# Indexer scores head by head, with query and key/value projections between the heads, and the first attention scores of layer 1 ahead of its last gate projection

## What is computed

```python
q, k, v, qi, ki, wi, z = jnp.split(h @ w_in, DSA_SPLITS, axis=-1)
q = rope(q.reshape(B, S, DSA_HEADS, DSA_HEAD_DIM), pos)      # 8 heads of 128
k = rope(k.reshape(B, S, DSA_KV_HEADS, DSA_HEAD_DIM), pos)
qi = rope(qi.reshape(B, S, IDX_HEADS, IDX_DIM), pos)         # 8 heads of 64
ki = rope(ki, pos)
logits = jnp.einsum('bqhd,bkd->bqhk', qi, k_idx) * (IDX_DIM ** -0.5)
score = jnp.einsum('bqhk,bqh->bqk', jax.nn.relu(logits), wi * (IDX_HEADS ** -0.5))
score = jnp.where(causal[None], score, -jnp.inf)
_, idx = lax.top_k(score, top_k)                             # top_k = 256
o = dsa_attention(...)        # softmax over the selected keys only
return (o * jax.nn.silu(z)) @ w_out
```

## Time and profile before

| | |
|---|---|
| time, median of 3 runs | 1346.89 us (1346.02 to 1347.38) |
| the profiled execution | 1348.37 us, its span 1346.5 us |
| PE busy | 1302.9 us, 97% of the span |
| DVE, ACT, POOL busy | 803.5, 563.1, 524.6 us |
| chain that ended last | PE 38% of the span, DVE 5%, ACT 2%, POOL 1% |
| mean granted clock of PE | 0.99 |

### The profile page before, as it was taken

How to read it: one execution, slowest core, us unless ns; L and a number is a source line. 1 busy time by engine, 2 the same in 40 slices (tenths; PEclk the granted TensorE clock), 3 DMA queues, 4 the chain that set the end, 5 groups by cost and what they waited for, 6 DMA issues and landing times. The chain is left out here.

```text
span 1346.5 us, 19019 instructions
## 1 busy us (share of the span) xinstructions
PE 1302.9 (97%) x6890; PEld 1111.5 (83%) x6890; DVE 803.5 (60%) x1581; ACT 563.1 (42%) x1134; POOL 524.6 (39%) x721
## 2 busy tenths in 40 slices
PE   9999999999999999999987999999899999999997
PEld 8878888989898888888766788888788988888885
DVE  7624755555556345245577889977977776345233
ACT  8312244554454023123235665564266666023122
POOL 2842034554443744234401132331066564744201
PEclk9999999999999999999998999999999999999999
DMA  6232331121101522133300122342222221521122
GB/s 203 77 106 78 112 116 56 55 71 48 55 32 56 175 87 75 60 96 120 95 0 1 55 87 89 110 140 67 88 72 64 79 63 64 153 95 59 60 65 87
DMA packets 83372, 110.07 MB, mean 82 GB/s; under 512 B 9552, under 2 KB 45648, under 8 KB 83280
## 3 DMA queue, kind: packets, MB, share of 16 engines
q1 hardware_dynamic: 83280, 108.86, 26.0%
HBM read 81.04 MB, written 27.79 MB: 81 GB/s over the span
## 5 line engine op out<-in xcount | busy, mean ns | idle before, releaser
L1700 PE MATMUL psum<-ring_hi,act_lo 128*128 128x512 f32 x816 | 322.4, 395 | 0.7 <-DVE act_lo L1688 0.7
L1702 PE MATMUL psum<-ring_hi,act_hi 128*128 128x512 f32 x816 | 318.9, 391 | 0.0
L1701 PE MATMUL psum<-ring_lo,act_hi 128*128 128x512 f32 x816 | 318.8, 391 | 0.0
L1126 POOL CAST ring_hi<-raw 128x512 fp32r<-128x512 f32 x128 | 81.8, 639 | 322.6 <-DMA raw<-in_dsa_w_in 144.0
L1341 DVE TENSOR_TENSOR act_lo<-psum,act_hi 128x512 fp32r<-128x512 f32 (+3 forms) x276 | 156.0, 594 | 67.2 <-ACT act_hi L1170 40.9
L1129 POOL TENSOR_TENSOR ring_lo<-raw,ring_hi 128x512 fp32r<-128x512 f32 x128 | 180.0, 1406 | 10.4
L1700 PEld LDWEIGHTS psum<-ring_hi,act_lo 128*128 128x128 f32 x816 | 154.1, 189 | 32.8 <-DVE act_lo L1688 1.4
L1702 PEld LDWEIGHTS psum<-ring_hi,act_hi 128*128 128x128 f32 x816 | 153.8, 188 | 32.3
L1701 PEld LDWEIGHTS psum<-ring_lo,act_hi 128*128 128x128 f32 x816 | 154.1, 189 | 31.0
L1170 ACT ACTIVATE act_hi<-psum 128x512 fp32r<-128x512 f32 (+1 forms) x244 | 114.9, 511 | 150.2 <-PE psum L1912 80.5
L1140 POOL TENSOR_TENSOR small<-small 128x1 f32<-128x1 f32 x128 | 70.7, 552 | 228.7 <-ACT p L1308 169.8
(11 more groups left out here) (257 smaller groups left out, 2473.7 us busy)
## 6 DMA issues: line engine op xcount, KB each, us to landing
raw<-in_dsa_w_in SPq DMA_DIRECT2D x48, 256.0 KB, 3.1
gz<-z_scratch SPq DMA_DIRECT2D x16, 512.0 KB, 3.6
raw<-in_ple_w_gate SPq DMA_DIRECT2D x32, 256.0 KB, 3.1
raw<-in_mla_w_in SPq DMA_DIRECT2D x19, 256.0 KB, 2.9
xr<-in_x_t SPq DMA_DIRECT2D x16, 256.0 KB, 6.8
z_scratch<-gz SPq DMA_DIRECT2D x16, 256.0 KB, 2.0
raw<-in_mla_w_out SPq DMA_DIRECT2D x16, 256.0 KB, 3.4
p<-in_x SPq DMA_DIRECT2D x16, 256.0 KB, 3.1
```

Source lines behind the costliest of these rows:

```text
L1126: last = nc.gpsimd.tensor_copy(dst, src[:, c0:c0 + cols])
L1700: nc.tensor.matmul(dst, lhs(1), rhs(0), start=start, stop=False)
L1701: nc.tensor.matmul(dst, lhs(0), rhs(1), start=False, stop=False)
L1702: return nc.tensor.matmul(dst, lhs(0), rhs(0), start=False, stop=stop)
```

## The change

In the indexer each head is a step of its own, with one bank (or a pair of banks over 512 keys), taken in turn from rings B and A. There are three rows for relu copies instead of two, the third in `xr`. The projection of tile t + 2 stands behind head 1 of tile t, the split of tile t + 1 behind head 5. In tiles 6 and 7, where no query projection is left, key/value projections 0 and 1 stand in that place. The rotated query rows go to a place of their own in `xr`, so `p1` is free for the key/value rows.

The search uses DVE on tiles 2, 3 and 4 and ACT on 5, 6 and 7; gate jobs 2 and 5 carry two rounds. The last step counts on DVE only for ACT's tiles. `above` is gone: ACT makes sign(threshold - score) of each tile with its sum, and DVE works the selection in three passes and one of a single column. The tiles are selected in the order 6, 4, 7, 3, 5, 2.

Key transposes of group 0 move behind gate job 12, the value split behind job 13, and behind job 14 stand two masks (in `xr`), the scores, minimum and Exp of tiles 6 and 7 of head 0 and the selection of tile 2. Gate job 15 takes its bank from ring B and writes its result to `xr` instead of to `p0`. Keys and values of layer 1 lie in halves of the activation buffer that the last gate jobs no longer read. Two weight pieces of the output projection are fetched at gate jobs 9 and 11.

```diff
-SEARCH = [2, 4, 5, 3, 6, 7]
-ACT_TILES = [3, 6, 7]
+SEARCH = [2, 3, 4, 5, 6, 7]
+ACT_TILES = [5, 6, 7]
+KV_EARLY = 2
+TWO_ROUNDS = (2, 5)
+SELECT = [6, 4, 7, 3, 5, 2]
...
+    def idx_scores(t, heads):
         keys = (t + 1) * P
-        for h in range(0, IDX_HEADS, 2):
-            wide = keys > CW
-            s = add("idx", {"b_full": 2, "relu": 2, "sc": 2}, ring="AB"[h // 2 % 2], jobs=2, freed=["relu"],
...
+        for h in heads:
+            add("idx", {"b_full": 1, "relu": 1, "sc": 1}, ring=next_ring(), jobs=1, freed=["relu"],
+                wide=keys > CW, t=t, h=h, keys=keys, q_ready=max(qi_ready[t], lo_at["kiT"]),
+                x2=now["x2_st"], gfree=read_by["G"])
...
+    qi_job(FULL + 2)
+    kv_weights(6, 7)
+    idx_scores(FULL, range(4))
+    qi_split(FULL + 1, next_ring())
+    idx_scores(FULL, range(4, IDX_HEADS))
+    add("idx_mask", None, t=FULL)
+    for t in range(FULL + 1, T):
+        idx_scores(t, range(2))
+        if t + 2 < T:
+            qi_job(t + 2, next_ring())
+        elif t - T + 2 < KV_EARLY:
+            kv_job(t - T + 2, next_ring())
+        idx_scores(t, range(2, 6))
         if t + 1 < T:
-            qi_ready[t + 1] = qi_split(t + 1, rot[t + 1])
-        if t + 2 < T:
-            rot[t + 2] = qi_job(t + 2)
-        idx_scores(t, qi_ready[t])
+            qi_split(t + 1, next_ring())
+        idx_scores(t, range(6, IDX_HEADS))
+        add("idx_mask", None, t=t)
...
-    after_bits = [("last_step", None, {}), ("above", None, {})]
-    after_bits += [("sel", {"found": 1}, {"t": t}) for t in range(FULL, T)]
+    after_bits = [("last_step", {"thr": 1}, {})]
+    after_bits += [("sel", {"found": 1, "sgn": 1}, {"t": t, "side_free": max(0, j - 1)}) for j, t in enumerate(SELECT)]
...
     def z_extra(k):
         search()
+        if k in TWO_ROUNDS:
+            search()
...
+        if k == 12:
+            for j in range(2):
+                k_ready[0] = split4("p1", 0, ("k0_ld", k0.after["k0_ld"]), dest="kT", g=0, j=j).after["lo"]
+        if k == 13:
+            first_q["next"] = t2_load("q", 1, v_prep(0, first_q["v_ld"], now["a_full"]))
+        if k in (9, 11):
+            w(chunk_of(1, 7), k // 2 - 4)
...
+        if k == 14:
+            for qb in order[:2]:
+                add("mask_first", None, t=qb)
+            for qb in order[:2]:
+                ps = att["n"] % 3
+                early.append((0, qb, e_step(s_step(1, 0, qb, max(first_q["ready"], k_ready[0]), first=True)), ps))
+            kind, incs, kw = after_bits.pop(0)
+            add(kind, incs, **kw)
+            p0_stored.extend(gate_free[j] for j in range(2))
...
+                    nc.scalar.activation(side_at(t), score_at(t), ACT.Sign, bias=u_cand.bitcast(F32)[:, i:i + 1],
+                                         scale=-1.0, accum_out=cnt[:, i:i + 1]).then_inc(sem["sgn"], 1)
...
                     linked(nc.vector.tensor_scalar(eq, score_at(t), thr, None, ALU.is_equal))
-                    linked(nc.vector.tensor_tensor_scan(order, eq, eq, 0.0, ALU.add, ALU.max))
-                    linked(nc.vector.scalar_tensor_tensor(eq, order, need[:, i:i + 1], eq, ALU.is_le, ALU.mult))
-                    nc.vector.scalar_tensor_tensor(score_at(t), score_at(t), thr, eq, ALU.is_gt,
-                                                   ALU.add).then_inc(sem["found"], 1)
+                    linked(nc.vector.tensor_tensor_scan(order, eq, eq, float(2 * keys - 4 * TOPK), ALU.add, ALU.add))
+                    dve.wait_ge(sem["sgn"], s.after["sgn"])
+                    linked(nc.vector.scalar_tensor_tensor(need[:, i:i + 1], order[:, keys - 1:keys], 0.5, cnt[:, i:i + 1],
+                                                          ALU.mult, ALU.add))
+                    nc.vector.scalar_tensor_tensor(score_at(t), order, need[:, i:i + 1], side_at(t), ALU.is_le,
+                                                   ALU.is_gt).then_inc(sem["found"], 1)
```

More of the change, by code:

```diff
@@ L260, in z_chunk @@
             else:
-                proj(lay, i, job, ["zs"], {"zs": 1, "z_st%d" % slot: 1}, slot=slot, base=base)
+                proj(lay, i, job, ["zs"], {"zs": 1, "z_st%d" % slot: 1}, slot=slot, base=base,
+                     side_read=now["found"], ring="B" if base and job == 7 else "A")
+                gate_free[slot] = now["z_st%d" % slot]
             if extra:
@@ L626, in qi_split, with qi_job @@
[L626 to L631, removed]
+    rot, qi_ready, stack_read = {}, {}, {}
+    def qi_job(t, ring="A"):
+        rot[t] = rope_job(1, 1, t, t % 2, cs=cs.after["cs_ld"], stack_read=stack_read.get(t - 2), ring=ring,
+                          x2=now["x2_st"]).after["rot"]
@@ new lines, in qi_split, with kv_job, kv_weights @@
+    def qi_split(t, ring="B"):
+        s = add("qi_split", {"b_full": 2, "hi": 2, "lo": 2}, ring=ring, jobs=2, freed=["lo"], slot=t % 2, rot=rot[t])
+        stack_read[t] = s.after["hi"]
+        qi_ready[t] = s.after["lo"]
+    def kv_job(t, ring="A"):
+        slot = t % 2
+        rope_job(1, 2, t, slot, extra_inc={"st%d" % slot: 1, "vcopy": 1}, st_before=now["st%d" % slot], ring=ring)
+    def kv_weights(*rows):
+        for d in rows:
+            w(next_chunk(1, 1), d)
+    kv_weights(0, 1)
@@ L663, in search @@
         search_end(search_begin())
-    n = 0
-    for i, name in ((2, "kv"), (3, "q"), (4, "q")):
+    for t in range(KV_EARLY, T):
+        for job in range(KV_EARLY) if t == KV_EARLY else ():
+            ahead(next_chunk(1, 2), job)
+        ahead(next_chunk(1, 2), t)
+        kv_job(t)
+        search()
+    for i in (3, 4):
         for t in range(T):
             ahead(next_chunk(1, i), t)
[L669 to L679, removed]
+            slot = t % 2
+            st = search_begin()
+            rope_job(1, i, t, slot, extra_inc={"st%d" % slot: 1}, base=(i - 3) * CW, st_before=now["st%d" % slot])
+            search_end(st)
     q_stored = (now["st0"], now["st1"])
@@ L713, in plan @@
     act_free = now["a_full"]
-    k_ready, v_ready = {}, {}
-    for j in range(2):
-        k_ready[0] = split4("p1", 0, ("k0_ld", k0.after["k0_ld"]), dest="kT", g=0, j=j).after["lo"]
-    def v_prep(g, ld, act_free):
-        s = add("v_split", {"hi": 1, "lo": 1}, g=g, ld=ld, act_free=act_free)
-        v_ready[g] = s.after["lo"]
-        return ("lo", s.after["lo"])
-    rd = v_prep(0, first_q["v_ld"], act_free)
-    waiting = []
+    ld = first_q["next"]
+    waiting = list(early)
     ready_pv = []
@@ L1667, in _ @@
                     else:
-                        nc.vector.tensor_tensor_reduce(rows[ps][:, 0:keys], src, mask_at(n["qb"]).bitcast(F32),
+                        if n["z_done"]:
+                            dve.wait_ge(sem["z_st0"], n["z_done"][0])
+                            dve.wait_ge(sem["z_st1"], n["z_done"][1])
+                        mask = mask_first(n["qb"]) if n["first"] else mask_at(n["qb"]).bitcast(F32)
+                        nc.vector.tensor_tensor_reduce(rows[ps][:, 0:keys], src, mask,
                                                        -DSA_SCALE, 3.4e38, ALU.add, ALU.min,
```

201 lines of the change are left out of this document (116 added, 85 removed).

## The result

The changed kernel takes 1349.34 us (median, 1345.91 to 1351.93) against 1347.47 us before (1346.02 to 1348.61): ratio 1.0013, 95% interval 1.0007 to 1.0018. So the changed kernel is 0.9 to 2.4 us slower, where 11.4 us less were forecast. The profiled execution took 1349.3 us, the median itself, around a span of 1347.5 us.

The account below looks back on a forecast made before the run. TensorE was taken as the bound, busy 1302.9 of 1346.5 us. Gains of 4.4 (indexer), 0 (search) and 7.0 us (head 0) sum to 11.4, giving 1335.5 us; bounds 1328.0 to 1343.5 us.

Parts of the forecast that it names:

- Part 3: Start of head 0 of layer 1's attention: PE's waits and lowered clock go, less 1.6 us new wait; -7.0 us.
- half rate: Indexer: PE waits of 2 us or more bring 3.3 us at half clock; 3.6 x 1.65 = 5.9 us.
- Part 1: Indexer, heads unpaired and two key/value projections moved among them: 10.3 us gained at full clock, -4.4 us after lowered clock.
- chain forecast: Indexer, one projection's end to the next: rotation, accumulates, split, two heads, projection; 12.9 to 15.4 us a tile.
- Part 2: Search during projections and gate jobs: PE never waits for it, DVE's last selection comes in time; 0 us.
- rival B: Search late: rounds beside Silu take 5.3 us, not 4.3, shrinking head 0's gain to 2 to 3; about 1340 us, chance 0.18.
- Rival C: Nothing to measure: five halved clocks in the indexer and a wait for row 0 in head 0; 1344 to 1349 us, 0.08.
- row chain: Head 0, from a score in PSUM to its scaled row: 4.1 us, fitting beside the last gate job's 5.44 us.
- Rivals A and D: Indexer. A: clock stays up, 1329.6 us, chance 0.20. D: lower clock covers whole projections, 1357 us, chance 0.07.

Follow-up runs that it names:

- both repairs: Changed kernel with the next tile's query split put ahead of the projection and the weight piece fetched at gate job 13; 1327.45 us, ratio 0.9851.

## Why the prediction was wrong

**Part 3 failed, and took most of the forecast.** It took the first scores, exponentials and scaling as the whole path of head 0 and asked of SP only whether the gate rows come in time for their reader ("the first output that wants them comes behind six more scores, so 0"). That is true of the reader and not of the queue. The weight piece stands behind that load on SP, and its cast stands in POOL's order between two rows that PE waits for. Rows brought forward by 6 us overtook a transfer that was pushed back by 1.7. The price is 7.3 us in head 0 (234.0 against 226.7 with the piece ahead): PE stands idle 5.0 us longer (6.9 against 2.0) and is busy 2.4 us longer (227.1 against 224.7), at half rate. Without it part 3 is worth 6.1 us where 7.0 were forecast; of new waits the forecast took 1.6 us for row 0, and there are two for splits on DVE, 0.4 and 0.6 us. Of the 6.1, only 2.3 to 2.8 are due to the early scores.

**Part 1 had the mechanism right and a term too small.** From one projection's end to the next (the first from 671.82), at the forecast's own split into chain and half rate:

| projection behind heads 0, 1 of tile | 3 | 4 | 5 | 6 | 7 |
|---|---|---|---|---|---|
| chain forecast, us | 12.9 | 14.15 | 14.7 | 15.4 | 15.4 |
| measured, us | 13.4 | 16.2 | 15.2 | 17.3 | 19.0 |
| of it half rate (half the stretch) | 0 | 1.6 | 0 | 1.6 | 3.0 |
| measured chain | 13.4 | 14.6 | 15.2 | 15.7 | 16.0 |

Each link is 0.3 to 0.6 us longer, 2.2 us in all. Of these 1.3 us are DVE's own pause between its accumulates, 0.12 us where 0.04 were taken, which the forecast named as its lower end (16 x 0.1 us) and left out. The other 0.9 lie between the projection's end and the first accumulate, 2.87 us where 2.75 were taken in four links and 2.36 for 1.95 in the last. For example, behind the projection that ends at 685.19 DVE's split begins at 691.49, 6.3 us later, where 2.75 + 3.16 = 5.9 were taken. In DVE's timeline (a row of two, with 0.12 us between):
```profile
689.82 1.64 DVE L1651 SCALAR_TENSOR_TENSOR xr<-gz,wis,xr 128x512 f32<-128x512 f32 x2
691.49 1.30 DVE L1430 TENSOR_TENSOR head_w_hi<-psum,head_w_hi 64x512 fp32r<-64x512 f32 x2
```
Half rate cost 6.2 us for 5.9 forecast, but in three stretches, one of them 6.0 us long, not in 3.6 of 3.3. So part 1 gave 2.1 us in this execution, inside its bounds of 0.4 and 10.3 us. That the half rate came out so near is luck: with the same waits PE was busy up to 3.1 us longer in the other kernels' profiles. The trace of the kernel before already spoke against the forecast's rule that a wait of 2 us or more is followed by half rate. Its four stretches are the indexer's; the wait of 2.04 us at 970.15 is followed by full rate:
```profile
971.49 0.40 PE L1700 MATMUL psum<-act_hi,kpe_lo 128*128 128x512 f32 x1
```

**What the forecast did not ask** was whether the order of the chain was needed. It worked out that the new order stands still for 14.6 us and took this as its nature. The split reads rotated rows that are there one tile earlier; ahead of the projection it costs nothing, and 13.3 us of the indexer go.

**Part 2** was right: 0, and the last selection is in time; rival B did not happen. Rival C (1344 to 1349 us at 0.08) came nearest in its number, 0.3 us below the measured time, and not in its mechanism, since part 3 did not come near its lower end of 3.0 but fell below 0, which its bounds excluded: they were drawn from the row chain alone. Rivals A and D did not happen.

Of the 1.9 us outside both parts, 0.9 lie ahead of the changed code, where the profiled executions of the kernels here vary between 664.0 and 665.6 us. The 0.9 us behind head 1's first score also stand in the experiments' profiles (354.7 to 355.3 us against 354.3); their cause was not looked for and stays open.

## What to carry to other kernels

When rows on the critical path are brought forward, list for every in-order queue that they pass, POOL and SP too, what stands between two of them, and when its transfer is issued: a cast that has always been ready is so only by the old lateness. A load that waits for a store holds everything behind it on its queue (1.7 us here); fetch what others wait for ahead of it. And where a forecast finds a chain of latencies, ask for each step when its input is there: a step whose input is a tile old can be put down ahead of the long work. The value of an edit depends on which bound is left, 0 or 5.8 us for the same two lines here.

## What the runs showed of the hardware

The same wait at the same place is followed by a half rate in one profile and not in another. PE's wait for the low half of tile 3's split, in the changed kernel and in the one with the split ahead:
```profile
679.30 0.39 PE L1973 MATMUL psum<-kpe_lo,head_w_lo 128*128 128x512 f32 x1
```
```profile
677.71 0.60 PE L1972 MATMUL psum<-kpe_lo,head_w_lo 128*128 128x512 f32 x1 [1.84 <-DVE head_w_lo L1429]
678.11 0.63 PE L1972 MATMUL psum<-kpe_hi,head_w_lo 128*128 128x512 f32 x1
```
The waits are 1.85 and 1.84 us. Ten of the profiles here have this wait; six show the half rate behind it and four do not. The wait of 2.00 us before tile 5's first head is alike: full rate in the changed kernel, half rate in the one with the piece ahead, whose next projection takes 7.0 us instead of 5.5. In the kernel with the projections behind the heads a wait of 2.49 us was followed by full rate. PE worked at half rate for 3.1 to 6.2 us behind one wait in the indexer. So a forecast of one stretch per wait of about 2 us is a chance and not a count. It fits that the changed kernel's 20 times spread over 6.0 us with mean clocks between 0.988 (slowest) and 0.992 (fastest), and that its indexer differs by 3.1 us between profiles by half rate alone. The kernel with both repairs, with few such waits, spreads over 1.8 us, but in four runs only, and the kernel before, with six waits of 1.96 to 2.93 us, over 2.6 us in 20; that the stretches make the whole spread was not tested by itself.

The table loads on ACT at the last gate job:
```profile
970.81 0.97 ACT L1245 ACTIVATE act_hi<-psum 128x512 fp32r<-128x512 f32 x2
971.80 1.28 ACT L1396 ACT_TABLE_LOAD   x1
973.10 0.40 ACT L1396 ACTIVATE p<-p,small 128x128 f32<-128x128 f32 x1
```
The load takes 1.28 us, with 0.02 us ahead of it and 0.02 us behind. The Trainium skill, ScalarE: Activation LUTs (What ACT_TABLE_LOAD costs), adds a drain of about 1.38 us to each switch; an estimate by that figure puts the row of tile 0 at 974.5 us. Where ACT was at work up to the load, as here, the trace shows no such drain.
